# Forgetting gates summed by a scan on turned rows instead of by matmuls, in a two-layer decoder kernel

## The chip, the cores and the metric

The kernel runs on one core of one Trainium2 chip. Its time is the device time of one launch, in microseconds, median of several runs. It works in float32; TensorE gets rounded halves of each operand (a high part and the rest, type fp32r), so every large product is three matmuls.

## The reference

Two decoder layers on an input of 256 rows by 1024 columns. Each layer projects the normalised input to 7428 columns (pool input, queries, keys and values of three attentions, 4 forget logits, 4096 gate logits), runs four mixers, gates and sums them, and then a SwiGLU. What matters here is the forgetting attention with 4 heads:

```
log_f = jax.nn.log_sigmoid(f_logit.astype(jnp.float32) + b_forget.astype(jnp.float32))
cum = jnp.cumsum(log_f, axis=1).transpose(0, 2, 1)
...
logits = (jnp.einsum('bhqd,bhkd->bhqk', qb, k).astype(jnp.float32) * scale
          + cq[..., :, None] - cum[..., None, :])
```

The sum runs over the 256 positions, one per head; the logits need it once by query and once by key.

## The kernel before

**Units.** All large products are cut into 144 units a layer (lists `ITEMS`, `UNITS`). A unit is two slices of 128 rows of a weight matrix by 512 columns, and TensorE does 12 matmuls for it. For each unit SyncE loads 512 KB into one of 6 buffers `raw`, ScalarE writes the rounded part `w_hi` (L884), VectorE writes the rest `w_lo` (L1175), and both wait for a ring of 5: `w_hi` of unit u+4 is written in step u, once TensorE has finished unit u-1. Results stand in `bulk`, two pairs of PSUM banks that items use in turn: the first matmul of an item waits until the item two before has been read out of its bank. The item `gate 6` begins with unit 52, and its bank is given back when VectorE has read item `gate 4` (`gate(layer, 4)`, L1500).

**Order.** Every engine works through its own list, written by hand: `MIXING_PE`, `MIXING_ACT` and `MIXING_DVE` give the step (unit) before which a stage is done. An engine does its stages strictly in that order and waits at each for its semaphores. After the stages of step u, ScalarE and VectorE prepare unit u+4. SyncE's queue carries the weight loads and the trips through device memory (`ROWS_AT`, `PROBS_AT`: steps of going out and of coming back).

**Forgetting gates.** VectorE's `fox_forget` (step 29, L1336) ends the softplus: 128 positions by 8 columns (2 tiles, 4 heads). TensorE's `cum` (step 35, L1711 and L1712) multiplies it by constant triangles, and `cum_evac` on VectorE (step 32 of its list, L1353 to L1357) splits the result into a rounded part and a rest, beside columns of ones that GpSimd filled once. `tr_forget` (step 37, L1695) transposes these rows with four matmuls into bank T, and ScalarE's `forget_evac` (L1034, L1035) copies them as four-row operands `forgetsT` into `queries_hi` and `keys_hi`. `scores("fox", h)` on TensorE (steps 42 and 47) adds the product of these four rows to the scores.

**What follows on ScalarE and VectorE.** `softmax("diff", 3)` and `fox_evac` (steps 38 and 39) prepare the queries and keys of the forgetting attention. Then come `maxima("fox", 0)`, `softmax("fox", 0)`, the copies `o_d` of the differential attention, GpSimd's squares of them (L837), `diff_norm`, `maxima("fox", 1)`, `softmax("fox", 1)`, the three sigmoids of step 48 (L1071), `w_hi` and `w_lo` of unit 52, and `gate(layer, 4)`.

**Turn of the queries.** `turn("dq")` transposes 32 by 32 blocks on VectorE (L1545), SyncE writes them to device memory (L616) and reads them back (L623), and `qk_evac("dq")` reads them in step 23 (ScalarE L962). `lambdas` is three operations on single columns of VectorE.

Of the kernel before, what the change touches and what calls it, by code (L numbers as in the profile page):

```python
# [24 lines left out]
F32 = mybir.dt.float32  # L25
F32R = mybir.dt.float32r
# [6 lines left out]
P = 128  # L33
TT = 2
# [98 lines left out]
def timetable(*entries):  # L133
# [22 lines left out]
def stage_parts(stage, *args):  # L156
# [6 lines left out]
    if stage in ("cum", "pool_a", "pool_b", "tr_forget"):  # L163
        return [((stage,), "T")]
# [26 lines left out]
TURN_AT = {"dq": 13, "dk": 17, "fox": 33, "diff": 48, "merged": 62}  # L191
SPREAD_AT = {}
D0 = LAST[("down", 0)] + 1
ROWS_AT = {"dq": (17, 18), "fox": (36, 37), "diff": (50, 51), "merged": (66, 68), ("ffn", 0): (F0 + 1, F0 + 2), "norm": (D0 + 4, D0 + 5)}
# [8 lines left out]
for _s, _at in PROBS_AT.items():  # L203
# [13 lines left out]
    (32, "softmax", "diff", 1), (34, "probs_evac", "diff", 0), (36, "softmax", "diff", 2), (37, "forget_evac"),  # L217
    (38, "softmax", "diff", 3), (39, "fox_evac", "fq"), (39, "fox_evac", "fk"), (41, "probs_evac", "diff", 1),
# [14 lines left out]
    (37, "probs_turn", "diff", 2), (37, "maxima", "diff", 3), (39, "softmax", "diff", 3), (39, "probs_turn", "diff", 3),
    (39, "fox_evac", "fq"), (39, "fox_evac", "fk"), (40, "gate", 2), (41, "pv_evac", "diff", 1), (41, "maxima", "fox", 0),
    (41, "softmax", "fox", 0), (41, "probs_turn", "fox", 0), (44, "pv_evac", "diff", 2), (44, "gate", 3),
    (45, "pv_evac", "diff", 3), (46, "diff_norm"), (46, "turn", "diff"), (47, "maxima", "fox", 1), (48, "softmax", "fox", 1),
    (48, "probs_turn", "fox", 1), (49, "gate", 4), (49, "pool_evac_b"), (52, "gate", 5), (55, "diff_evac", 1),
    (55, "diff_evac", 0), (56, "gate", 6), (57, "pv_evac", "fox", 0), (57, "pv_evac", "fox", 1), (63, "turn", "merged"),
    (69, "merged_evac", 0), (69, "gate", 7), (71, "merged_evac", 1)]
# [53 lines left out]
def constant_blocks():  # L293
# [6 lines left out]
    blocks["minus_upto"] = (key <= col) * -1.0  # L300
    blocks["minus_ones"] = -np.ones((P, P))
# [20 lines left out]
def build(nc, x, attn_norm, ffn_norm, w_in, b_gate, w_branch, w_out, w_ffn_up, w_ffn_down, consts, params, turned_x, out):  # L322
# [8 lines left out]
    with ExitStack() as ctx:  # L331
# [76 lines left out]
        forget_rows = sb("forget_rows", [P, P + 16], F32, mixing)  # L408
        forget_window = {(w, t): forget_rows[:, 8 * i + 4 * t:8 * i + 4 * t + P] for i, w in enumerate(("fq", "fk")) for t in range(TT)}
# [1625 lines left out]
```

## Time and profile before

| | us |
|---|---|
| median of 3 runs (832.94 to 833.03) | 833.02 |
| the profiled execution | 832.95 |
| its span | 831.1 |
| TensorE busy, 3974 matmuls | 825.6 (99%) |
| VectorE busy | 636.8 (77%) |
| ScalarE busy | 445.8 (54%) |
| GpSimd busy | 200.0 (24%) |

The profiled execution is 1.85 us longer than its span. TensorE's granted clock stands at its upper level (2.4 GHz) in all 40 slices of the page. The two layers follow one another: layer 0 runs to about 411 us of the span, and what layer 0 does at 163 us layer 1 does at 574 us. A line of the timeline gives start, busy time, engine, line, operation, tiles and shapes, how many were merged, and in brackets how long the engine sat idle before it and who released it. Matmuls overlap, so their durations add up to more than the time that passes; the distance between two starts is what a matmul costs TensorE.

### The profile page before, as it was taken

The numbers are of one execution on the slowest core, as the hardware profiler recorded it, in microseconds if no ns is written. First come the engines' busy times: TensorE is split into PE (matmuls) and PEld (weight loads), VectorE is DVE, ScalarE is ACT, GpSimd is POOL, SyncE is SP. The second block draws the span as 40 slices with busy tenths as digits, with TensorE's granted clock in tenths as the row PEclk, the third lists the DMA queues.
The fourth block names the chain that finished last, engine by engine and source line by source line (L and its number), as shares of the span: only waits on it lengthen the run. The fifth ranks groups of instructions, "written<-read, shape, count | busy, mean of one in ns | idle before, by whom it ended". The sixth has DMA issues, their size and how long they took to land.

```text
span 831.1 us, 11025 instructions
## 1 busy us (share of the span) xinstructions
PE 825.6 (99%) x3974; PEld 682.1 (82%) x3974; DVE 636.8 (77%) x958; ACT 445.8 (54%) x642; POOL 200.0 (24%) x285
## 2 busy tenths in 40 slices
PE   9999999999999999999999999999999999999998
PEld 8878788788888888888888888887888888888887
DVE  7899988799687676664679989977986876666652
ACT  6656756654554445444375676566543645444441
POOL 0601201008112333343005102010361133333400
PEclk9999999999999999999999999999999999999999
DMA  9878798686676777676666787886876777776641
GB/s 338 289 227 268 215 293 255 222 280 225 210 239 233 249 214 219 218 228 189 188 216 187 229 252 223 258 275 220 267 243 199 214 244 218 221 219 222 211 141 50
DMA packets 114486, 189.24 MB, mean 228 GB/s; under 512 B 17152, under 2 KB 35072, under 8 KB 114432
## 3 DMA queue, kind: packets, MB, share of 16 engines
q1 hardware_dynamic: 106768, 178.96, 68.3%
q0 software_dynamic: 7232, 8.93, 3.4%
q10 hardware_dynamic: 432, 0.66, 0.3%
q8 instruction: 31, 0.51, 0.2%
q14 instruction: 23, 0.19, 0.1%
HBM read 170.14 MB, written 12.58 MB: 220 GB/s over the span
## 4 chain that ended last, share of the span: by engine, by line
PE 92%; DVE 3%; DMA 2%; ACT 1%; issue 1%; SPq 1%; ACTq 0%; DVEq 0%
PE bulk L1883 29%; PE bulk L1887 29%; PE bulk L1884 29%; DMA raw<-in_w_in_dram 2%; PE bankAB L1676 2%; DVE w_lo L1175 2%; PE bankAB L1792 0%; ACT wide L1071 0%; ACT w_hi L884 0%; PE bankO L1803 0%; PE bankO L1804 0%; PE bankO L1805 0%; PE bankT L1733 0%; SPq L682 0%; SPq L693 0%
## 5 line engine op out<-in xcount | busy, mean ns | idle before, releaser
L1175 DVE TENSOR_TENSOR w_lo<-raw,w_hi 128x1024 fp32r<-128x1024 f32 (+1 forms) x288 | 358.3, 1260 | 110.1 <-ACT w_hi L884 107.5
L884 ACT ACTIVATE w_hi<-raw 128x1024 fp32r<-128x1024 f32 (+1 forms) x286 | 297.0, 1048 | 262.0 <-PE bulk L1887 255.5
L1883 PE MATMUL bulk<-w_hi,hT_hi 128*128 128x512 f32 (+1 forms) x880 | 342.4, 389 | 1.9 <-DVE wide L1286 1.1
L1884 PE MATMUL bulk<-w_lo,hT_hi 128*128 128x512 f32 (+1 forms) x880 | 339.4, 386 | 0.0
L1887 PE MATMUL bulk<-w_hi,hT_lo 128*128 128x512 f32 (+1 forms) x880 | 336.4, 386 | 0.0
L1883 PEld LDWEIGHTS bulk<-w_hi,hT_hi 128*128 128x128 f32 x880 | 165.3, 188 | 36.7 <-issue 2.2
L1887 PEld LDWEIGHTS bulk<-w_hi,hT_lo 128*128 128x128 f32 x880 | 165.0, 188 | 33.3
L1884 PEld LDWEIGHTS bulk<-w_lo,hT_hi 128*128 128x128 f32 x880 | 165.3, 188 | 32.0
L860 POOL DMA_DIRECT2D wide<-wide x192 | 95.0, 504 | 172.1 <-DVE wide L1545 169.7
L846 POOL TENSOR_TENSOR wide<-wide 128x512 f32<-128x512 f32 x24 | 46.1, 1942 | 100.6 <-DVE wide L1510 100.1
L1884 PE MATMUL bulk<-w_lo,aT_hi 128*128 128x512 f32 x174 | 67.8, 389 | 0.0
L1887 PE MATMUL bulk<-w_hi,aT_lo 128*128 128x512 f32 x174 | 67.7, 389 | 0.0
L1883 PE MATMUL bulk<-w_hi,aT_hi 128*128 128x512 f32 x174 | 67.7, 389 | 0.0
L1883 PEld LDWEIGHTS bulk<-w_hi,aT_hi 128*128 128x128 f32 x174 | 32.7, 188 | 6.8
L1887 PEld LDWEIGHTS bulk<-w_hi,aT_lo 128*128 128x128 f32 x174 | 32.7, 188 | 6.7
L1884 PEld LDWEIGHTS bulk<-w_lo,aT_hi 128*128 128x128 f32 x174 | 32.7, 188 | 6.7
L1883 PE MATMUL bulk<-w_hi,oT_hi 128*128 128x512 f32 x80 | 31.4, 392 | 0.0
L1884 PE MATMUL bulk<-w_lo,oT_hi 128*128 128x512 f32 x80 | 31.2, 390 | 0.0
L1887 PE MATMUL bulk<-w_hi,oT_lo 128*128 128x512 f32 x80 | 31.1, 389 | 0.0
L1044 ACT ACTIVATE sb<-bankAB,nmx 128x256 f32<-128x256 f32 x24 | 11.4, 473 | 30.8 <-DVE nmx L1423 30.7
L837 POOL TENSOR_TENSOR wide<-o_d 128x512 f32<-128x512 f32 x4 | 5.9, 1492 | 85.8 <-DVE o_d L1456 85.8
L1528 DVE SCALAR_TENSOR_TENSOR wide<-bulk,y_ffn,wide 128x512 f32<-128x512 f32 (+1 forms) x24 | 15.8, 701 | 10.2 <-ACT wide L1099 10.2
(240 smaller groups left out, 711.3 us busy)
## 6 DMA issues: line engine op xcount, KB each, us to landing
raw<-in_w_in_dram SPq DMA_DIRECT2D x110, 512.0 KB, 4.9
raw<-in_w_ffn_up_dram SPq DMA_DIRECT2D x80, 512.0 KB, 4.6
raw<-in_w_ffn_down_dram SPq DMA_DIRECT2D x44, 512.0 KB, 3.8
raw<-in_w_branch_dram SPq DMA_DIRECT2D x20, 512.0 KB, 5.1
raw<-in_w_out_dram SPq DMA_DIRECT2D x16, 512.0 KB, 3.7
wide<-wide POOLq DMA_DIRECT2D x160, 32.0 KB, 3.3
bias<-in_b_gate_dram SPq DMA_DIRECT2D x16, 256.0 KB, 4.7
raw<-in_w_ffn_up_dram SPq DMA_DIRECT2D x16, 256.0 KB, 3.4
```

Of the source, the lines that this page charges most:

```text
L837: last = pool.tensor_tensor(scratch(t, TA).rearrange("p (h d) -> p h d", h=4), o_d[:, t, :, :], o_d[:, t, :, :], ALU.mult)
L846: ins = pool.tensor_tensor(m, m, wide[:, t, n * D + j * NC:n * D + (j + 1) * NC], ALU.add)
L860: pool.dma_start(spread[b * QUAD:(b + 1) * QUAD, a, :, 0:blocks, :], turned[a * QUAD:(a + 1) * QUAD, b, :, 0:blocks, :]).then_inc(block_sp ...
L884: act.activation(w_hi[:, g % RING, :, 0:width], raw[:, g % RAW, :, 0:width], ACT.Copy).then_inc(hi_ready, 1)
L1044: act.activation(expd[:, m, P:P + SEQ], bank[b][:, P:P + SEQ], ACT.Exp, bias=nmx[:, m:m + 1], accum_out=den[:, m:m + 1])
L1175: vec.tensor_tensor(w_lo[:, g % RING, :, 0:width], raw[:, g % RAW, :, 0:width], w_hi[:, g % RING, :, 0:width].bitcast(F32), ALU.subtract). ...
L1528: vec.scalar_tensor_tensor(out=s, in0=item_bank(layer, ITEM_AT[item], t)[:, 0:width], scalar=y_ffn[:, t:t + 1], in1=s, op0=ALU.mult, op1=A ...
L1676: ins = pe.matmul(dst, a[a_part], b[b_part], start=start and a_part + b_part == 0, stop=stop and a_part == 1, skip_group_check=True)
L1883: pe.matmul(dst, hi, whi, start=(k == ks[0]), stop=False)
L1884: pe.matmul(dst, hi, wlo, start=False, stop=False)
L1887: ins = pe.matmul(dst, lo, whi, start=False, stop=(k == ks[-1] or g == DEPTH * U - 2 and i == 1 and t == 1))
```

## The change

The sum over the positions is no longer made by TensorE.

- `fox_forget` writes the softplus into a 128 x 32 tile and VectorE transposes that in 32 x 32 blocks.
- GpSimd, behind its multiplication `fox_gain` (L823), sends the 128 x 32 tile to device memory, waits for it, and reads it back with 8 transfers so that head h stands on partitions 32h to 32h+3 with all 256 positions in a row (`cumulated`).
- VectorE's new stage `forget_cum`, behind `maxima("diff", 3)`, sums along the row with one scan.
- The new stage `forget_split` on ScalarE (three operations of 128 x 256, the second and third waiting for the first) and on VectorE (three of 128 x 256) makes the rounded part and the rest and writes the four-row operands with signs and ones from a small constant table. It stands behind `softmax("diff", 3)` on ScalarE and behind `fox_evac` on VectorE.
- `cum`, `cum_evac`, `tr_forget` and `forget_evac` are gone.
- `turn("dq")` comes after `qk_norm("dk")` instead of before it, its way out one step later (17 to 18), its way back two (18 to 20); `lambdas` goes from step 10 to step 20.

```diff
-TURN_AT = {"dq": 13, "dk": 17, "fox": 33, "diff": 48, "merged": 62}
+TURN_AT = {"dq": 14, "dk": 17, "fox": 33, "diff": 48, "merged": 62}
...
-ROWS_AT = {"dq": (17, 18), "fox": (36, 37), ...
+ROWS_AT = {"dq": (18, 20), "fox": (36, 37), ...
...
+                pool.wait_ge(forget_turned, nth(forget_turned, layer, "rows"))
+                pool.dma_start(dram_forget.rearrange("a c j -> (a c) j"), forget_rows[:, 1, :]).then_inc(forget_out, 16)
+                pool.wait_ge(forget_out, 16 * nth(forget_out, layer, "rows"))
+                for r in range(4):
+                    for t in range(TT):
+                        pool.dma_start(cumulated[r::QUAD, t * P:(t + 1) * P].rearrange("h (a j) -> h a j", a=NQUAD),
+                                       dram_forget[:, 4 * t:4 * t + 4, :].rearrange("a h j -> h a j")).then_inc(forget_back, 16)
...
-            def forget_evac(layer):
-
-                act.wait_ge(stage_done, nth(stage_done, layer, ("tr_forget",)))
-                act.activation(forgetsT["fq"], bank["T"][:, 0:SEQ], ACT.Copy)
-                act.activation(forgetsT["fk"], bank["T"][:, SEQ:2 * SEQ], ACT.Copy).then_inc(forgetsT_ready, 1)
+            def forget_split(layer):
+
+                act.wait_ge(cum_ready, nth(cum_ready, layer, "cum"))
+                act.wait_ge(stage_done, nth(stage_done, layer, ("scores", "diff", 3)))
+                act.activation(cum_hi, cumulated, ACT.Copy).then_inc(cum_split, 1)
+                act.wait_ge(cum_split, nth(cum_split, layer, "high"))
+                sign, one = c("forget_rows")[:, 0:6:3], c("forget_rows")[:, 2:6:3]
+                for i, which in enumerate(("fq", "fk")):
+                    act.activation(forgetsT[which], cum_hi.bitcast(F32), ACT.Identity, bias=one[:, i:i + 1],
+                                   scale=sign[:, i:i + 1]).then_inc(cum_split, 1)
...
-                vec.scalar_tensor_tensor(out=fg[:, 4, :], in0=fg[:, 0, :], scalar=0.0, in1=fg[:, 3, :],
-                                         op0=ALU.max, op1=ALU.add).then_inc(forget_out, 1)
+                vec.scalar_tensor_tensor(out=softplus, in0=fg[:, 0, :], scalar=0.0, in1=fg[:, 3, :],
+                                         op0=ALU.max, op1=ALU.add).then_inc(vec_step, 1)
+                vec.wait_ge(vec_step, count_step())
+                if layer:
+                    vec.wait_ge(forget_out, 16 * nth(forget_out, layer - 1, "rows"))
+                vec.transpose(forget_rows[:, 1, :], forget_rows[:, 0, :]).then_inc(forget_turned, 1)
...
-            def cum_evac(layer):
...
+            def forget_cum(layer):
+
+                vec.wait_ge(forget_back, 16 * 8 * nth(forget_back, layer, "rows"))
+                vec.tensor_tensor_scan(cumulated, cumulated, cumulated, 0.0, op0=ALU.add, op1=ALU.max).then_inc(cum_ready, 1)
+
+            def forget_split(layer):
+
+                vec.wait_ge(cum_split, nth(cum_split, layer, "high"))
+                vec.tensor_tensor(cum_lo, cumulated, cum_hi.bitcast(F32), ALU.subtract).then_inc(vec_step, 1)
                 vec.wait_ge(vec_step, count_step())
+                sign = c("forget_rows")[:, 1:6:3]
+                for i, which in enumerate(("fq", "fk")):
+                    vec.wait_ge(cum_split, nth(cum_split, layer, "queries" if which == "fq" else "keys"))
+                    last = vec.scalar_tensor_tensor(out=forgetsT[which], in0=cum_lo.bitcast(F32), scalar=sign[:, i:i + 1],
+                                                    in1=forgetsT[which].bitcast(F32), op0=ALU.mult, op1=ALU.add)
+                last.then_inc(forgetsT_ready, 1)
...
-            def tr_forget(layer):
...
-            def cum(layer):
```

Where it lands in the engines' programs. ScalarE of layer 0, before, around step 37: `w_hi` is L884, the softmax of the differential head 3 is L1044 and L1046, `forget_evac` L1034 and L1035, `fox_evac` L1028.

```order
82 L884 ACTIVATE w_hi<-raw 128x1024
83 L1034 ACTIVATE queries_hi<-bankT 128x256
84 L1035 ACTIVATE keys_hi<-bankT 128x256
85 L884 ACTIVATE w_hi<-raw 128x1024
86 L1044 ACTIVATE sb,den<-bankAB,nmx 128x256
87 L1046 ACTIVATE sb,den<-bankAB,nmx 128x128
88 L1044 ACTIVATE sb,den<-bankAB,nmx 128x256
89 L1046 ACTIVATE sb,den<-bankAB,nmx 128x128
90 L884 ACTIVATE w_hi<-raw 128x1024
91 L1028 ACTIVATE queries_hi<-wide 128x2x128 x2
```

The same place now (`w_hi` L891, softmax L1056 and L1058, `forget_split` L1042 and L1046, `fox_evac` L1035):

```order
82 L891 ACTIVATE w_hi<-raw 128x1024 x2
83 L1056 ACTIVATE sb,den<-bankAB,nmx 128x256
84 L1058 ACTIVATE sb,den<-bankAB,nmx 128x128
85 L1056 ACTIVATE sb,den<-bankAB,nmx 128x256
86 L1058 ACTIVATE sb,den<-bankAB,nmx 128x128
87 L1042 ACTIVATE queries_lo<-wide 128x256
88 L1046 ACTIVATE queries_hi<-queries_lo,con 128x256
89 L1046 ACTIVATE keys_hi<-queries_lo,con 128x256
90 L891 ACTIVATE w_hi<-raw 128x1024
91 L1035 ACTIVATE queries_hi<-wide 128x2x128 x2
```

Two operations in front of the softmax have become three behind it, in front of `w_hi` of unit 42.

VectorE of layer 0 at steps 32 and 33, before: `gate 0` (L1500), `cum_evac` (L1353 to L1357), `w_lo` of unit 36 (L1175), the maxima of the differential head 2.

```order
473 L1500 SCALAR_TENSOR_TENSOR wide<-bulk,y_attn,bias 128x512 x2
474 L1353 CAST forget_rows<-bankT 128x2x4
475 L1355 TENSOR_TENSOR forget_rows<-bankT,forget_rows 128x2x4
476 L1357 TENSOR_SCALAR forget_rows<-forget_rows 128x2x4x2
477 L1175 TENSOR_TENSOR w_lo<-raw,w_hi 128x1024
478 L1420 TENSOR_REDUCE row_max<-bankAB 128x2
479 L1421 TENSOR_REDUCE row_max<-bankAB 128x2
```

Now:

```order
472 L1521 SCALAR_TENSOR_TENSOR wide<-bulk,y_attn,bias 128x512 x2
473 L1187 TENSOR_TENSOR w_lo<-raw,w_hi 128x1024
474 L1441 TENSOR_REDUCE row_max<-bankAB 128x2
475 L1442 TENSOR_REDUCE row_max<-bankAB 128x2
```

The three small operations, and the wait for TensorE in front of them, are gone.

VectorE of layer 0 at step 39, before: the end of the softmax, the block transpose of the probabilities (L1579), `fox_evac` (L1399), `w_lo` of unit 43, `gate 2`.

```order
502 L1444 SCALAR_TENSOR_TENSOR probs_room<-sb,inverse,probs_room 128x128
503 L1579 STREAM_TRANSPOSE wide<-probs_room 128x3x4x32
504 L1399 TENSOR_TENSOR queries_lo<-wide,queries_hi 128x2x128 x2
505 L1399 TENSOR_TENSOR keys_lo<-wide,keys_hi 128x2x128 x2
506 L1175 TENSOR_TENSOR w_lo<-raw,w_hi 128x1024
507 L1500 SCALAR_TENSOR_TENSOR wide<-bulk,y_attn,bias 128x512 x2
```

Now:

```order
499 L1465 SCALAR_TENSOR_TENSOR probs_room<-sb,inverse,probs_room 128x128
500 L1600 STREAM_TRANSPOSE wide<-probs_room 128x3x4x32
501 L1420 TENSOR_TENSOR queries_lo<-wide,queries_hi 128x2x128 x2
502 L1420 TENSOR_TENSOR keys_lo<-wide,keys_hi 128x2x128 x2
503 L1372 TENSOR_TENSOR keys_lo<-wide,queries_lo 128x256
504 L1377 SCALAR_TENSOR_TENSOR queries_hi<-keys_lo,con,queries_hi 128x256
505 L1377 SCALAR_TENSOR_TENSOR keys_hi<-keys_lo,con,keys_hi 128x256
506 L1187 TENSOR_TENSOR w_lo<-raw,w_hi 128x1024
507 L1521 SCALAR_TENSOR_TENSOR wide<-bulk,y_attn,bias 128x512 x2
```

Three operations of 256 columns stand between `fox_evac` and `w_lo` of unit 43.

## Rows read from the trace of the kernel before

**Rows 1.** Waits of TensorE, whole span: us in total, times, longest.

```profile
PE bulk L1883 <- DVE wide L1500: 0.8, 2, 0.4
```

**Rows 2.** Timeline of TensorE, layer 0: start, busy, line, shapes, count.

```profile
105.31 0.28 PE L1711 MATMUL bankT<-fg,con 128*128 128x8 f32 x2
...
105.74 0.39 PE L1676 MATMUL bankAB<-keys_hi,queries_hi 64*128 64x256 f32 x2
...
106.59 0.39 PE L1792 MATMUL bankAB<-masks 128*128 128x256 bf16 x2
...
114.13 0.60 PE L1695 MATMUL bankT<-con,forget_rows 128*128 128x128 f32 x4
114.48 0.48 PE L1883 MATMUL bulk<-w_hi,hT_hi 128*128 128x512 f32 x1
...
117.32 0.39 PE L1883 MATMUL bulk<-w_hi,hT_hi 128*128 128x512 f32 x1
...
163.34 0.47 PE L1883 MATMUL bulk<-w_hi,hT_hi 128*128 128x512 f32 x1 [0.41 <-DVE wide L1500]
```

**Rows 3.** Timeline of VectorE, layer 0: the same columns.

```profile
71.84 0.70 DVE L1175 TENSOR_TENSOR w_lo<-raw,w_hi 128x520 fp32r<-128x520 f32 x1 [1.04 <-ACT w_hi L884]
...
95.08 0.70 DVE L1336 SCALAR_TENSOR_TENSOR fg<-fg 128x8 f32<-128x8 f32 x1
...
105.85 0.17 DVE L1353 CAST forget_rows<-bankT 128x8 fp32r<-128x8 f32 x1 [0.86 <-PE bankT L1712]
...
106.35 1.22 DVE L1175 TENSOR_TENSOR w_lo<-raw,w_hi 128x1024 fp32r<-128x1024 f32 x1
107.48 0.68 DVE L1420 TENSOR_REDUCE row_max<-bankAB 128x2 f32<-128x512 f32 x1
...
122.25 1.23 DVE L1175 TENSOR_TENSOR w_lo<-raw,w_hi 128x1024 fp32r<-128x1024 f32 x1 [1.61 <-ACT w_hi L884]
...
124.45 0.48 DVE L1442 SCALAR_TENSOR_TENSOR probs_room<-sb,inverse,probs_room 128x256 f32<-128x256 f32 x1
...
127.04 1.22 DVE L1175 TENSOR_TENSOR w_lo<-raw,w_hi 128x1024 fp32r<-128x1024 f32 x1
...
133.97 0.18 DVE L1433 RECIPROCAL inverse<-den 128x4 f32<-128x4 f32 x1 [1.78 <-ACT sb L1046]
...
145.81 1.28 DVE L1465 TENSOR_REDUCE stat<-wide 128x4 f32<-128x512 f32 x2 [1.93 <-POOL wide L837]
...
161.30 1.23 DVE L1175 TENSOR_TENSOR w_lo<-raw,w_hi 128x1024 fp32r<-128x1024 f32 x1 [2.92 <-ACT w_hi L884]
```

**Rows 4.** Timeline of ScalarE, layer 0.

```profile
71.71 1.14 ACT L962 ACTIVATE queries_hi<-probs_room 128x512 fp32r<-128x512 f32 x2
...
89.78 0.84 ACT L1001 ACTIVATE wide<-bulk,y_attn 128x256 f32<-128x256 f32 x2 [2.23 <-DVE fg L1322]
...
119.55 0.47 ACT L1044 ACTIVATE sb<-bankAB,nmx 128x256 f32<-128x256 f32 x1 [3.17 <-DVE nmx L1423]
...
121.14 1.07 ACT L884 ACTIVATE w_hi<-raw 128x1024 fp32r<-128x1024 f32 x1
...
154.34 0.47 ACT L1044 ACTIVATE sb<-bankAB,nmx 128x256 f32<-128x256 f32 x1 [4.99 <-DVE nmx L1423]
...
157.37 2.96 ACT L1071 ACTIVATE wide<-wide 128x1024 f32<-128x1024 f32 x3
```

**Rows 5.** Timeline of GpSimd, layer 0.

```profile
66.77 2.19 POOL L623 DMA_DIRECT2D wide<-rows_dk  x4 [3.33 <-DMA rows_dk<-wide]
94.64 5.31 POOL L823 TENSOR_TENSOR fox_gained<-wide,parameters 128x256 f32<-128x256 f32 x4 [25.68 <-DVE wide L1286]
```

**Rows 6.** Line L623: from issue to landing.

```profile
DMA to landing us min/median/max: 2.2/3.3/7.1
```

**Rows 7.** Line L1372, VectorE's scans: ns min/median/max.

```profile
L1372 DVE TENSOR_TENSOR_SCAN sb<-sb x16: 392/528/683, 64.5 to 488.6; 128x255 f32<-128x255 f32 x8, 128x127 f32<-128x127 f32 x8
```

**Rows 8.** Timeline of SyncE's queue, layer 0.

```profile
55.83 1.89 SPq L623 DMA_DIRECT2D probs_room<-rows_dq  x4
```

More of the change, by code:

```diff
@@ L229 @@
+    (19, "sb_turn", 0), (20, "lambdas"), (23, "qk_evac", "dq"), (24, "qk_evac", "dk"), (24, "sb_weights", 1),
     (24, "sb_turn", 1), (25, "maxima", "diff", 0), (27, "softmax", "diff", 0), (27, "probs_turn", "diff", 0), (29, "pf"),
     (29, "fox_norm"), (29, "fox_forget"), (30, "maxima", "diff", 1), (31, "sb_evac", 0), (32, "softmax", "diff", 1),
-    (32, "probs_turn", "diff", 1), (32, "sb_evac", 1), (32, "gate", 0), (32, "cum_evac"), (33, "maxima", "diff", 2),
-    (33, "turn", "fox"), (36, "pv_evac", "diff", 0), (36, "gate", 1), (37, "softmax", "diff", 2),
@@ L233 @@
[L233 to L237, printed above, removed]
@@ L238 @@
-    (55, "diff_evac", 0), (56, "gate", 6), (57, "pv_evac", "fox", 0), (57, "pv_evac", "fox", 1), (63, "turn", "merged"),
-    (69, "merged_evac", 0), (69, "gate", 7), (71, "merged_evac", 1)]
+    (32, "probs_turn", "diff", 1), (32, "sb_evac", 1), (32, "gate", 0), (33, "maxima", "diff", 2), (33, "turn", "fox"),
+    (36, "pv_evac", "diff", 0), (36, "gate", 1), (37, "softmax", "diff", 2), (37, "probs_turn", "diff", 2),
+    (37, "maxima", "diff", 3), (37, "forget_cum"), (39, "softmax", "diff", 3), (39, "probs_turn", "diff", 3),
@@ new lines @@
+    (39, "fox_evac", "fq"), (39, "fox_evac", "fk"), (39, "forget_split"), (40, "gate", 2), (41, "pv_evac", "diff", 1),
+    (41, "maxima", "fox", 0), (41, "softmax", "fox", 0), (41, "probs_turn", "fox", 0), (44, "pv_evac", "diff", 2),
+    (44, "gate", 3), (45, "pv_evac", "diff", 3), (46, "diff_norm"), (46, "turn", "diff"), (47, "maxima", "fox", 1),
+    (48, "softmax", "fox", 1), (48, "probs_turn", "fox", 1), (49, "gate", 4), (49, "pool_evac_b"), (52, "gate", 5),
+    (55, "diff_evac", 1), (55, "diff_evac", 0), (56, "gate", 6), (57, "pv_evac", "fox", 0), (57, "pv_evac", "fox", 1),
@@ L243, in evacuations @@
+    (63, "turn", "merged"), (69, "merged_evac", 0), (69, "gate", 7), (71, "merged_evac", 1)]
 def evacuations(mixing, *branches):
@@ L546, in build @@
         forget_ln = signal("forget_ln", ["ln"])
-        forget_out = signal("forget_out", ["softplus", "aug"])
+        forget_turned = signal("forget_turned", ["rows"])
+        forget_out, forget_back = signal("forget_out", ["rows"]), signal("forget_back", ["rows"])
+        cum_ready, cum_split = signal("cum_ready", ["cum"]), signal("cum_split", ["high", "queries", "keys"])
         pooled = signal("pooled", ["pooled"])
@@ L1686, in tr_norm @@
                 ins.then_inc(stage_done, 1)
-            def tr_forget(layer):
-                pe.wait_ge(forget_out, nth(forget_out, layer, "aug"))
-                take("T", forgetsT_ready, layer, "both")
-                for i, which in enumerate(("fq", "fk")):
-                    for t in range(TT):
-                        at = i * SEQ + t * P
-                        ins = pe.transpose(bank["T"][:, at:at + P], forget_window[which, t], identity)
-                ins.then_inc(stage_done, 1)
             def tr_ss(layer):
@@ L1704, in tr_ss @@
                     ins.then_inc(stage_done, 1)
-            def cum(layer):
-                pe.wait_ge(forget_out, nth(forget_out, layer, "softplus"))
-                take("T", forget_out, layer, "aug")
-                sp = fg[:, 4, :]
-                pe.matmul(bank["T"][:, 0:8], c("minus_upto"), sp, start=True, stop=False, skip_group_check=True)
-                ins = pe.matmul(bank["T"][:, 4:8], c("minus_ones"), sp[:, 0:4], start=False, stop=True, skip_group_check=True)
-                ins.then_inc(stage_done, 1)
             def pool_a(layer):
```

58 lines of the change are left out of this document (23 added, 35 removed).

## The prediction, made before the changed kernel ran

> **What bounds the kernel now.** The table of the page comes first: TensorE is busy 99% of the span, so a matmul less is worth its time only where TensorE is never made to wait afterwards. So the second view is TensorE's waits. They are short, but one comes once in each layer and from the same place: 0.41 us until VectorE has read `gate 4` [rows 1, 2]. That is the first matmul of unit 52, at 163.34 us. TensorE was there early; VectorE was late. The third view is therefore the timeline of VectorE, read backwards from there, and what ended each of its idle times.
>
> `w_lo` of unit 52 starts at 161.30, after 2.92 us of idle, released by ScalarE's `w_hi` [rows 3]. ScalarE wrote that behind the three sigmoids of 157.37, these behind a table load and the softmax of 154.34, and that had waited 4.99 us for VectorE's maxima [rows 4]. Before it VectorE idled at 145.81 for GpSimd's squares of a tile that VectorE itself had written, at 133.97 for ScalarE's softmax, and at 122.25 for `w_hi`, which stood behind the softmax that began at 119.55 on VectorE's maxima [rows 3, 4]. None of these waits was ended by TensorE or by a transfer. Going back, the first idle time that TensorE ends is 105.85: 0.86 us for `cum` [rows 3]. So from 105.85 to 163.34 a rigid chain of VectorE, ScalarE and GpSimd runs beside TensorE and is the later of the two when they meet. Call its shift by the change d. TensorE leaves unit 52 d later than before, whatever it saved ahead of it, as long as d is above minus 0.8 (below that its own work binds). Behind unit 52 nothing makes TensorE wait until the next layer, so d is what the layer's time changes by.
>
> **The change part by part.** I work in layer 0; layer 1 has the same wait [rows 1].
>
> *TensorE.* `cum` takes from 105.31 to 105.74, 0.43 us; the four transposes from 114.13 to 114.48, 0.35 us [rows 2]. TensorE is 0.43 us earlier behind step 35 and 0.78 us earlier behind step 37. By the last paragraph this is worth nothing as such: the wait before unit 52 grows by it.
>
> The transposes' rows show 0.60 us for four together [rows 2], while their starts leave 0.35 us to the next product. The Trainium skill ("TensorE: Matmul & The Clock Gate", PE-mode transpose) gives some 275 ns for one transpose of 128 x 128 in a kernel. Four would be 1.1 us an estimate, and the saving 1.5 us a layer; the row disagrees, since these overlap, and the row decides.
>
> *The start of the chain.* VectorE loses 0.86 us of waiting and the three operations of `cum_evac`, which together take from 105.85 to 106.35, 0.50 us [rows 3]. In return the new block transpose stands behind the softplus at 95.08. Its price is not in the trace. Small operations take 0.17 us, but the softplus itself took 0.70 us there, beside GpSimd's multiplication of 94.64 [rows 3, 5]; so 0.2 to 0.7 us, and I take 0.5. Then `w_lo` of unit 36 ends, and the next maxima can start, at 107.48 - 1.36 + 0.5 = 106.6. The maxima also need TensorE's scores, whose last mask matmul began at 106.59, lasted 0.39, and comes 0.43 earlier: 106.55 plus a release [rows 2]. Both say 106.6 to 106.7 instead of 107.48: the chain starts 0.8 us earlier (0.7 to 0.9).
>
> *The scan.* It stands behind `maxima("diff", 3)`, whose successor on ScalarE, the softmax, is not held by it. Scans of 255 elements take at most 0.68 us [rows 7]. It lies in the 1.61 us that VectorE idles ahead of 122.25 [rows 3]; ScalarE needs its result only when the softmax has ended, 1.6 us later. Price 0, and up to 0.7 if that idle time were gone.
>
> *The trip through device memory.* GpSimd ends `fox_gain` at 94.64 + 5.31 = 99.95 [rows 5]. The way out takes an issue of some 0.55 and, as in the rows, 3.3 us of waiting; eight issues at 2.19/4 = 0.55 make 4.4; landing is 3.3 (at most 7.1) [rows 5, 6]. That is 111.5, and 119.1 with both ways at 7.1. The scan asks at 118.7 (0.8 before the 119.55 of the softmax behind the same maxima). Price 0 with 7 us to spare; at the worst 0.4 us. Behind these transfers GpSimd has nothing to do until the squares that release VectorE at 145.81 [rows 3].
>
> *ScalarE's half of the split.* Three operations of 256 columns with factors and offsets from a tile, the second waiting for the first, in front of `w_hi` of unit 42, with nothing ahead to wait for. The nearest row is L1001: two of 256 in 0.84 us [rows 4]. Three are 1.1 us (0.8 to 1.3). The old `forget_evac` stood ahead of the softmax in time that ScalarE spent waiting for the maxima (3.17 us before 119.55 [rows 4]), so its removal gives nothing back. `w_hi` of unit 42 starts at 121.14 - 0.8 + 1.1 = 121.4, and `w_lo`, which waits for it, is 0.3 us late.
>
> *VectorE's half.* Three operations of 256 columns between `fox_evac` and `w_lo` of unit 43 (127.04 [rows 3]), in front of which VectorE does not idle. The row L1442 of the same kind has 0.48 us [rows 3]; less the overlap of starts they are 1.2 us (1.0 to 1.4). Queued behind are `w_lo` of unit 43, `gate 2`, the copy `o_d` and `maxima("fox", 0)`: the whole rest of the chain.
>
> *The forgetting scores of step 42.* TensorE waits there for both halves, which end near 128.6, and could come near 128.2. This wait of some 0.5 us costs nothing by itself; it eats saved time that is lost at unit 52 anyhow.
>
> *The queries' turn and the lambdas.* `turn("dq")` and `lambdas` lie ahead of 105.85, where the chain starts anew, and no TensorE wait follows from them: VectorE idles 1.04 us at 71.84 [rows 3], more than three short operations take. The way back of the queries was issued at 55.83 and is read at 71.71 [rows 4, 8]. Two units later (a unit takes 2.84 us from 114.48 to 117.32 [rows 2]) it is issued near 61 to 63, and lands near 66, at most 70 [rows 6]. Price 0; if it were read late, ScalarE would wait a microsecond or two, and that too before 105.85.
>
> **Sum.** d = -0.8 + 1.1 + 1.2 = +1.5 us a layer; with the ends of the three prices 0.9 to 2.0. Two layers: +3.0 us on the profiled execution of 832.95 us (span 831.1 and 1.85 around it), which stands 0.07 below the median. I forecast 836.0 us, with a range of its own from 834.8 to 837.0.
>
> **The rivals.**
>
> *A, the matmuls' time is kept.* The new operations fall into idle time, d is at or below -0.8, and TensorE keeps 0.78 us a layer: 831.4 us. This is the other side. It decides at unit 52: there the chain must come forward by as much as TensorE does. For it: VectorE does idle 1.61 us just ahead. Against it: that idle time is ScalarE's work seen from VectorE, and the split lengthens just this work; and both halves stand where their engine does not wait.
>
> *B, only one half of the split lies on the chain.* Then d is 0.3 to 0.4, and the time 833.7 us. For it: the scan and ScalarE's half need not be strictly behind each other if ScalarE has idle time that I overlook. Against it: the 121.14 of `w_hi` follows the softmax directly.
>
> *C, the trip through device memory is late.* VectorE is stopped at the scan with everything behind it. If each of the nine issues had to wait for a VectorE operation of 1.2 us (the length of a `w_lo` [rows 3]), they would take 10.8 us in place of 5, the scan would ask before the data had landed at 99.95 + 10.8 + 7.1 + 7.1 = 125, and 6 us more a layer would give 848 us; with half that delay of the issues they land at 119.6, about 1 us late a layer, and the time is 838. Against it: the way of the keys, issued by the same engine, shows 0.55 us for each issue [rows 5]. The Trainium skill ("SBUF — State Buffer", SBUF: two separate sides) states this trap: a transfer issued by GpSimd needs its port to write descriptors, and VectorE can lock it. By that rule C would happen whenever VectorE runs operations that take the port; the four issues of the rows show no such delay.
>
> **Chances.** Forecast 0.80, B 0.08, A 0.07, C 0.05. A measurement of this kernel tells 0.2% (1.7 us) from no change. A ends just at that limit, B inside it; I give faster 0.05, no change 0.14, slower 0.81. The range is 833.9 to 837.4: down nearly to B, up beyond the bounds of d for a short delay by C.
>
> **What would show it.** In the new profile: TensorE's rows of the two groups gone; its wait before unit 52 near 2.2 us instead of 0.41 (0.41 + 1.5 late + 0.78 saved - 0.5 waited at step 42); `w_lo` of unit 42 0.3 us later than 122.25 and of unit 43 1.5 us later than 127.04; GpSimd's last read landed some 7 us before the scan; the scan not preceded by idle time for a transfer. I am wrong if unit 52 starts no later than 163.34, or if a transfer is what ends VectorE's wait.

## The result, and the profile after

The changed kernel takes 836.99 us (median of 6 runs, 836.14 to 839.76), the kernel before 833.00 (6 runs, 832.87 to 833.32). The ratio is 1.0054 with a 95% interval of 1.0044 to 1.0064: slower, as forecast, by 4.0 us where 3.0 were forecast. The median lies in the range, the direction and the place are those of the forecast; 3.1 us of the loss come from the path that the forecast priced (e1 below), and 0.9 us from the part that it priced at nothing. Something else was not foreseen: the runs of the kernel before agree within half a microsecond, those of the changed kernel lie 3.6 us apart.

The profiled execution of the changed kernel took 836.57 us, span 834.7. The page's busy times and its chain by engine:

```profile
PE 824.1 (99%) x3958; PEld 679.5 (81%) x3958; DVE 639.4 (77%) x962; ACT 446.5 (53%) x644; POOL 207.0 (25%) x301
...
PE 86%; DVE 8%; ACT 3%; issue 2%; POOL 1%; ACTq 0%; DVEq 0%
```

TensorE has 16 matmuls less and is busy 1.5 us less, but the chain that ended last passes through other engines for 14% of the span (8% before). Its waits, in the view of [rows 1]:

```profile
PE bankAB L1697 <- DVE keys_hi L1377: 3.1, 2, 2.0
PE bankO L1805 <- DVE o_d L1477: 2.1, 2, 1.0
PE bulk L1885 <- DVE wide L1521: 1.6, 2, 0.8
```

One wait of 0.4 us a layer has become three: for the new split at the forgetting scores of step 42, for a copy at step 45, for `gate 4` at unit 52. All three are releases of VectorE. Its timeline, the places of [rows 3] (maxima of head 2, the scan, `w_lo` of unit 42, the split, `w_lo` of units 43 and 52):

```profile
106.44 0.69 DVE L1441 TENSOR_REDUCE row_max<-bankAB 128x2 f32<-128x512 f32 x1
...
118.39 0.69 DVE L1367 TENSOR_TENSOR_SCAN wide<-wide 128x256 f32<-128x256 f32 x1
...
122.65 1.23 DVE L1187 TENSOR_TENSOR w_lo<-raw,w_hi 128x1024 fp32r<-128x1024 f32 x1 [2.46 <-ACT w_hi L891]
...
127.44 0.42 DVE L1372 TENSOR_TENSOR keys_lo<-wide,queries_lo 128x256 fp32r<-128x256 f32 x1
127.89 0.49 DVE L1377 SCALAR_TENSOR_TENSOR queries_hi<-keys_lo,con,queries_hi 128x256 fp32r<-128x256 f32 x1
128.30 0.48 DVE L1377 SCALAR_TENSOR_TENSOR keys_hi<-keys_lo,con,keys_hi 128x256 fp32r<-128x256 f32 x1
128.69 1.22 DVE L1187 TENSOR_TENSOR w_lo<-raw,w_hi 128x1024 fp32r<-128x1024 f32 x1
...
162.94 1.23 DVE L1187 TENSOR_TENSOR w_lo<-raw,w_hi 128x1024 fp32r<-128x1024 f32 x1 [2.92 <-ACT w_hi L891]
```

Against [rows 3] the maxima start 1.04 us earlier, `w_lo` of unit 42 starts 0.40 later, of unit 43 1.65 later, of unit 52 1.64 later. From unit 43 to unit 52 nothing changed. No row of the chain has a transfer as its releaser, and the scan starts straight behind the maxima. ScalarE's part, where [rows 4] had `w_hi` right behind the softmax:

```profile
120.11 0.43 ACT L1042 ACTIVATE queries_lo<-wide 128x256 fp32r<-128x256 f32 x1
120.57 0.60 ACT L1046 ACTIVATE queries_hi<-queries_lo,con 128x256 fp32r<-128x256 f32 x1
121.08 0.59 ACT L1046 ACTIVATE keys_hi<-queries_lo,con 128x256 fp32r<-128x256 f32 x1
121.57 1.04 ACT L891 ACTIVATE w_hi<-raw 128x1024 fp32r<-128x1024 f32 x1
```

From 120.11 to 121.57 the split holds `w_hi` back for 1.46 us. The sum of layer 0 is -1.04 + 1.46 + 1.24 = +1.66, which is the 1.64 of unit 52.

In layer 1, measured from TensorE's start of its unit 6, the same three terms are -0.76, +1.44 and +1.25, and unit 52 starts 1.95 us later.

GpSimd's trip through device memory (compare [rows 5]):

```profile
98.76 0.60 POOL L835 DMA_DIRECT2D rows_forget<-forget_rows  x1
101.39 4.52 POOL L839 DMA_DIRECT2D wide<-rows_forget  x8 [2.04 <-DMA rows_forget<-forget_rows]
```

The issues of the eight reads end at 105.9, and the last of them lands at 109.4, 9.0 us before the scan.

### The profile page after: what moved, and what is told of

The parts are those of the page before. It is cut to its first block, busy times and chain, and to the rows that moved or that the text cites. A ratio compares the mean times of both kernels' runs of the same rounds, so it can differ in the third digit from the quotient of the medians.

```text
span 834.7 us, 11016 instructions
## 1 busy us (share of the span) xinstructions
PE 824.1 (99%) x3958; PEld 679.5 (81%) x3958; DVE 639.4 (77%) x962; ACT 446.5 (53%) x644; POOL 207.0 (25%) x301
## 4 chain that ended last, share of the span: by engine, by line
PE 86%; DVE 8%; ACT 3%; issue 2%; POOL 1%; ACTq 0%; DVEq 0%
PE bulk L1885 27%; PE bulk L1889 27%; PE bulk L1886 27%; DVE w_lo L1187 2%; DVE wide L1521 1%; PE bankAB L1697 1%; POOL wide L844 1%; ACT w_hi L891 1%; PE bulk L1941 1%; ACT sb L1058 0%; ACT sb L1056 0%; PE bulk L1913 0%; PE bulk L1932 0%; PE bulk L1919 0%; DVE row_max L1441 0%
## 5 line engine op out<-in xcount | busy, mean ns | idle before, releaser
L891 ACT ACTIVATE w_hi<-raw 128x1024 fp32r<-128x1024 f32 (+1 forms) x286 | 296.8, 1047 | 264.8 <-PE bulk L1889 257.1
L1056 ACT ACTIVATE sb<-bankAB,nmx 128x256 f32<-128x256 f32 x24 | 11.4, 474 | 38.7 <-DVE nmx L1444 38.6
```

The costliest lines, as they stand in the source:

```text
L891: act.activation(w_hi[:, g % RING, :, 0:width], raw[:, g % RAW, :, 0:width], ACT.Copy).then_inc(hi_ready, 1)
L1056: act.activation(expd[:, m, P:P + SEQ], bank[b][:, P:P + SEQ], ACT.Exp, bias=nmx[:, m:m + 1], accum_out=den[:, m:m + 1])
```

## The experiments

All were timed in turns with the kernel before, which stood at 832.93, 832.99 and 833.03 us in the three groups (e1 to e4, e5 to e8, e9 to e12). The groups ran on two chips: e1 to e4 on one, e5 to e12 on another.

### e1 and e2: the change in two parts

**e1**, the gates' path alone:

```diff
-TURN_AT = {"dq": 14,          ROWS_AT = {"dq": (18, 20),
+TURN_AT = {"dq": 13,          ROWS_AT = {"dq": (17, 18),
-    (14, "qk_norm", "dk"), (14, "turn", "dq"), ... (20, "lambdas"),
+    (10, "lambdas"), (13, "turn", "dq"), (14, "qk_norm", "dk"), ...
```

> The changed kernel with the queries' turn back at step 13, their rows back at steps 17 and 18 and the lambdas back at step 10: only the forgetting gates' path is changed. Theory 1 (the chain of VectorE and ScalarE work up to unit 52 sets the time, everything ahead of it is slack): TensorE loses the 1.2 us that it gained before unit 16 of layer 0, waits that much less before unit 52 there, and the chain's shift per layer is that of layer 1 of the profiled run, +1.9 us: about 837 us, within 0.5 us of the changed kernel. Theory 2 (the later trip of the queries' rows to device memory is a part of the loss and makes the runs scatter): about 836 us, and the runs agree within 0.5 us where those of the changed kernel scatter over 3.6 us.

**e2**, the same lines the other way round in the kernel before:

> The kernel before with only the queries' turn, their rows' trip and the lambdas moved later; the forgetting gates stay on TensorE. Theory 1: TensorE's wait of 1.1 us before unit 16 of layer 0 goes, but the chain of VectorE starts earlier by no more than its wait for the cumulated sums (0.86 us) and TensorE gives the rest back before unit 52: 832.0 to 833.0 us. Theory 2: the later trip costs, 833.5 us or more, with runs that scatter.

e1: 836.06 us, five runs from 835.94 to 836.33, ratio 1.0038 (1.0026 to 1.0050). e2: 832.65 us, twelve runs from 831.95 to 839.32, ratio 1.0003 (0.9990 to 1.0016). So the gates' path costs 3.1 us, which is the forecast's sum, and its runs lie 0.4 us apart; the scatter belongs to the moved turn. Of the two expectations for e1 the second came true. The first took +1.9 us for each layer; in the profiled execution, counted from unit 6, unit 52 is 1.46 us late in layer 0 and 1.93 in layer 1. For e2 the median fits theory 1 and the scatter of 7.4 us theory 2: neither was whole. Its profiled execution (833.26 us) shows where lost time can come from, the first scores of TensorE waiting for the keys:

```profile
77.87 0.38 PE L1676 MATMUL bankAB<-keys_hi,queries_hi 64*128 64x256 f32 x2 [1.29 <-DVE keys_lo L1392]
```

### e5 and e6: which part of the move

The rows of the queries come back from device memory on SyncE's queue at step 20; GpSimd's queue sends the rows of the keys out at about the same time. **e5** moves the reads alone, in the kernel before:

```diff
-ROWS_AT = {"dq": (17, 18),
+ROWS_AT = {"dq": (17, 20),
```

> The kernel before with one number changed: the reads that bring the queries' rows back from device memory go out at step 20 of SyncE instead of 18, so that they run beside the write of the keys' rows by GpSimd. Theory 2 (the two trips share the DMA engines, the keys' rows land 1 to 3 us later, and in some runs TensorE waits for them at the first scores): runs that scatter over 2 us or more, from 832.9 us to 836 or more, mean 0.5 to 1.5 us above the kernel before. Rival (the turn behind the keys' norm, or the lambdas at step 20, make the scatter): 832.9 us, within 0.5 us in every run.

**e6** takes only that part out of the changed kernel:

```diff
-ROWS_AT = {"dq": (18, 20),
+ROWS_AT = {"dq": (17, 18),
```

> The changed kernel with only the two DMA steps of the queries' rows put back to 17 and 18; the turn stays behind the keys' norm and the lambdas stay at step 20. Theory 2: the reads are over before GpSimd writes the keys' rows, the scatter goes (all runs within 0.6 us), and the median is 836.0 us or up to 0.4 less, since TensorE's gain before unit 16 of layer 0 lets the chain start a little earlier. Rival (the later turn itself, or the trip of the gates' rows, makes the scatter): a median near 837 with runs over 1 us apart.

e5: 833.22 us, eleven runs from 832.85 to 834.39, ratio 1.0004 (0.9995 to 1.0013). e6: 835.46 us, seven runs from 835.12 to 836.07, ratio 1.0028 (1.0018 to 1.0039). e6 speaks for theory 2: with the two DMA steps back the runs lie 0.95 us apart instead of 3.6, though not within the 0.6 expected, and the median is 0.14 below the range expected. So the two DMA steps make the scatter, and neither the later turn nor the lambdas at step 20, which e6 keeps. With early rows the later turn is even worth 0.6 us against e1. e5 fell short of both of its expectations: its runs lie 1.5 us apart, where theory 2 said 2 or more and the rival 0.5, and its mean is 0.4 us above the median of the kernel before. The kernel before had 1.1 us between its own runs in that group, so the times of e5 alone show little.

The rows of the two queues say why the keys come late. In the changed kernel, layer 0, GpSimd's queue and then SyncE's (issue times, and GpSimd's wait for the way out before it asks for the way back):

```profile
61.62 0.76 POOL L619 DMA_DIRECT2D rows_dk<-wide  x1 [18.96 <-DVE wide L1566]
67.23 2.20 POOL L626 DMA_DIRECT2D wide<-rows_dk  x4 [4.85 <-DMA rows_dk<-wide]
...
61.04 1.89 SPq L626 DMA_DIRECT2D probs_room<-rows_dq  x4
```

In e6:

```profile
61.94 0.76 POOL L619 DMA_DIRECT2D rows_dk<-wide  x1 [18.95 <-DVE wide L1566]
66.00 2.19 POOL L626 DMA_DIRECT2D wide<-rows_dk  x4 [3.29 <-DMA rows_dk<-wide]
...
55.72 1.76 SPq L626 DMA_DIRECT2D probs_room<-rows_dq  x4
```

The queries' reads start to be issued 0.6 us ahead of the keys' write instead of 6 us ahead. What this does to the keys' transfers stands in the view of the transfers (KB each, median us from issue to landing). The changed kernel, from 50 to 88 us:

```profile
rows_dk<-wide POOLq DMA_DIRECT2D x1, 512.0 KB, 5.3
wide<-rows_dk POOLq DMA_DIRECT2D x4, 128.0 KB, 3.8
```

and e6:

```profile
rows_dk<-wide POOLq DMA_DIRECT2D x1, 512.0 KB, 3.8
wide<-rows_dk POOLq DMA_DIRECT2D x4, 128.0 KB, 2.9
```

The same view has the queries' reads at 4.0 us here and 2.9 in e6. The other profiled executions say the same. In the six with the reads at step 20 the keys' write took 4.7 to 5.3 us, in both layers. In the eight with the reads at step 18 it took 3.7 to 3.9 us in 14 of 16 cases, and 4.7 in layer 1 of e8 and of e9; so the queries' reads are the main cause of a slow write, but not the only one. The Trainium skill ("DMA: Bandwidth & Descriptors", Queues, rings and completion order) says that one DMA engine serves the queues it has work for in turn, packet by packet. These rows agree that the two queues slow each other, with 1.5 us for a write of 512 KB beside reads of 512 KB; the turns themselves no row shows.

The keys then land when ScalarE already wants them. ScalarE in the changed kernel:

```profile
74.48 1.16 ACT L969 ACTIVATE keys_hi<-wide 128x512 fp32r<-128x512 f32 x2 [1.38 <-DMA wide<-rows_dk]
```

Laid over each other, each layer from one of its first units, the profiled executions of e6 and of the changed kernel agree to 0.06 us in TensorE's starts of layer 1. In layer 0 `w_lo` of unit 28 is 1.40 us later, and units 42 to 60 are 1.2 us later. In the kernel before such a delay went under in the wait for `cum` [rows 3]. In e5 `w_lo` of unit 28 is 0.7 us later, counted from unit 6, and unit 52 0.06 later; of the wait of 0.86 us 0.25 is left:

```profile
105.76 0.17 DVE L1353 CAST forget_rows<-bankT 128x8 fp32r<-128x8 f32 x1 [0.25 <-PE bankT L1712]
```

The change took this wait away, and with it the slack behind which a late transfer could hide. In e2 the delay was larger, and 0.3 us of it reached unit 52.

### e12: the changed kernel once more

> The changed kernel as it is, once more. Theory 2: against the version with the queries' rows at steps 17 and 18 (835.46 us, runs within 0.95 us) it is 1 to 2 us slower and its runs lie over 2 us apart, and in its profile either w_lo of unit 28 comes over 1 us later or the first scores wait for the keys. Rival (its first six runs were chance): median within 0.5 us of 835.5.

839.75 us, five runs from 838.51 to 841.89, ratio 1.0086 (1.0072 to 1.0100): 4.3 us above e6 on the same chip, more than expected, above the range of the forecast, and its shortest run is longer than five of the first six. In its layer 1 the keys' rows released ScalarE after a wait of 1.8 us, TensorE's first scores waited 0.57, and the chain came 1.6 us late to the forgetting scores. There TensorE waited, and what followed was more than the wait (ScalarE's wait for the keys, then TensorE's at the forgetting scores):

```profile
488.23 1.16 ACT L969 ACTIVATE keys_hi<-wide 128x512 fp32r<-128x512 f32 x2 [1.80 <-DMA wide<-rows_dk]
...
542.89 0.58 PE L1697 MATMUL bankAB<-keys_hi,queries_hi 64*128 64x256 f32 x2 [2.00 <-DVE keys_hi L1377]
```

The same stretch by windows (length, busy time and count of PE, PEld, DVE, ACT, POOL, granted clock, DMA share, GB/s):

```profile
538.00:540.00 2.00, 2.00 (x11) 1.49 (x9) 1.92 (x6) 2.00 (x4) 0.00 (x0) 1.00 0.52 200
540.00:542.00 2.00, 0.89 (x7) 0.69 (x6) 1.97 (x6) 0.84 (x1) 0.00 (x0) 1.00 0.26 71
542.00:544.00 2.00, 1.11 (x11) 1.14 (x12) 2.00 (x4) 0.00 (x0) 0.00 (x0) 0.71 0.77 79
544.00:548.00 4.00, 4.00 (x18) 3.12 (x17) 3.54 (x7) 0.39 (x2) 0.00 (x0) 0.50 0.88 306
548.00:552.00 4.00, 4.00 (x16) 3.18 (x15) 2.57 (x8) 4.00 (x12) 0.00 (x0) 0.79 0.81 212
```

After the 2.00 us without work the granted clock fell to 0.50, its lower level (1.2 GHz), for 6.8 us. The unit behind the scores starts 2.6 us later than in e6, the next one 4.7, and at unit 52 it is still 3.15. Of the 3.15 us, 1.6 are the late keys, and I put the other 1.5 down to the clock, by subtraction; no run has the one without the other. The mean clock was 0.994 to 0.998 in all five runs of e12, and 1.000 in all 53 runs of the kernels with the reads at step 18 (e1, e6 to e11). It was 0.994 to 0.996 in four of the changed kernel's first six runs too, the shortest of them (836.14 us) and the longest (839.76) among the four, and 0.996 in the longest run of e2; in all runs of e3, e4 and e5 it was 1.000. So only kernels with late reads show the fall, not all of them do, and a fall does not have to make a run long. In the first profile a wait of the same 2.0 us, in layer 0, left the clock at 1.00, so the wait alone does not decide it. The Trainium skill ("TensorE: Matmul & The Clock Gate", What's actually happening) puts the clock down to how busy TensorE has been lately. The rows of e12 agree, with TensorE busy 0.89 of 2.00 us before the fall.

### e3 and e10: VectorE's half of the split

```diff
 def forget_split(layer):          # VectorE
-    vec.wait_ge(cum_split, nth(cum_split, layer, "high"))
-    vec.tensor_tensor(cum_lo, cumulated, ...)
-    ... two scalar_tensor_tensor into forgetsT
+    vec.wait_ge(cum_split, nth(cum_split, layer, "keys"))
+    vec.tensor_copy(nmx[:, 0:1], nmx[:, 0:1]).then_inc(forgetsT_ready, 1)
```

e3 is this edit in the changed kernel, e10 the same in e6.

> The changed kernel without VectorE's half of the split: the low parts of the cumulated sums are left out of the four rows (one operation of 4 elements stands in for the three of 256). Theory 1: the 1.24 us per layer of that half stand on the chain to unit 52, so it is 2 x 1.2 = 2.4 us (2.0 to 2.6) faster than the changed kernel, near 834.6. Rival (VectorE has slack there and the loss comes from the trip through device memory or from the clock): as the changed kernel within 0.5 us.

> The version with the queries' rows at steps 17 and 18 (835.46 us) without VectorE's half of the split: the low parts of the cumulated sums are left out of the four rows. The first try of this was clouded by the late rows. Theory 1: 2 x 1.24 us less, 833.0 us (832.7 to 833.3), with runs within 0.6 us. Rival (the half isn't on the path): 835.4.

e3: 834.60 us, eleven runs from 833.62 to 838.33, ratio 1.0026 (1.0017 to 1.0036). It is 2.4 us below the first median of the changed kernel, but with 4.7 us between its runs this shows little. e10: 832.97 us, eleven runs from 832.74 to 833.36, ratio 1.0000 (0.9991 to 1.0008): 2.49 us less than e6, 1.24 a layer, where 127.44 to 128.69 in the rows above is 1.25. (Laid over each other, the two profiled executions say 1.15 a layer; the small operation that stands in has a price too.)

### e4, e7 and e8: the same operations where their engines wait

The scan goes ahead of the softmax of head 2, ScalarE's half ahead of the exponentials of head 3 (5.8 us of waiting for the maxima), VectorE's half behind `w_lo` of unit 41 (2.5 us of waiting for `w_hi`):

```diff
 MIXING_DVE
-    (37, "maxima", "diff", 3), (37, "forget_cum"), ... (39, "fox_evac", "fk"), (39, "forget_split"),
+    (36, "forget_cum"), (37, "softmax", "diff", 2), ... (37, "maxima", "diff", 3), (38, "forget_split"),
 MIXING_ACT
-    (38, "softmax", "diff", 3), (38, "forget_split"),
+    (38, "forget_split"), (38, "softmax", "diff", 3),
 forget_split on ScalarE
-    act.wait_ge(stage_done, nth(stage_done, layer, ("scores", "diff", 3)))
+    act.wait_ge(stage_done, nth(stage_done, layer, ("scores", "diff", 2)))
```

e4 is this in the changed kernel, e7 in e1, e8 in e6.

> The changed kernel with the scan moved ahead of the softmax of head 2 (before it behind the maxima of head 3), ScalarE's half of the split ahead of the exponentials of head 3, where ScalarE waited 5.8 us, and VectorE's half behind w_lo of unit 41, where VectorE waited 2.5 us for w_hi of unit 42. Theory 1: of the chain's terms only the scan's 0.69 us is left beside the -1.04 of its start, so unit 52 starts 0.35 us per layer earlier than in the kernel before: 832.3 us (831.7 to 833.0), faster than both. Rival (the trip through device memory lands too late for a scan at 114 us in some runs, or the loss isn't these halves): 835 us or more, with scatter.

> The forgetting gates' path of the changed kernel with the queries' turn, rows and lambdas as before, and with the scan and both halves of the split moved into the idle times of ScalarE (5.8 us ahead of the exponentials of head 3) and VectorE (2.5 us ahead of w_lo of unit 42). Theory 1: per layer 1.46 + 1.24 us leave the chain and the scan's 0.69 us enters it, against the version with old turns and the split on the chain (836.06 us): 836.06 - 2 x 2.01 = 832.0 us (831.7 to 832.7), within 0.5 us in every run, 0.9 us faster than the kernel before. Rival (the chain to unit 52 is only as short as in the kernel before, because something else ends there): 832.9 us.

> As the one before, but with the queries' turn behind the keys' norm and the lambdas at step 20, the queries' rows at steps 17 and 18. Theory 1 and 2 together: TensorE loses the wait of 1.1 us before unit 16 of layer 0 and no run is late: 831.6 us (831.2 to 832.2), within 0.6 us in every run. Rival: as the one before or slower, with scatter.

e4: 832.61 us, eleven runs from 831.53 to 835.53, ratio 1.0000 (0.9992 to 1.0009), the median inside the range expected, with the scatter of the late reads; it was expected to be faster than the kernel before and is not. e7: 831.90 us, eleven runs from 831.62 to 832.02, ratio 0.9986 (0.9977 to 0.9995). e8: 830.99 us, nine runs from 830.86 to 831.33, ratio 0.9975 (0.9966 to 0.9985). e7 is 4.2 us below e1, where 4.0 were expected; e8 is 4.5 below e6 and 0.2 below the range expected for it. In e8 ScalarE runs its half in its waiting time, and 3 us of waiting are left ahead of the exponentials:

```profile
113.21 0.42 ACT L1042 ACTIVATE queries_lo<-wide 128x256 fp32r<-128x256 f32 x1 [0.81 <-DVE wide L1367]
...
117.77 0.47 ACT L1056 ACTIVATE sb<-bankAB,nmx 128x256 f32<-128x256 f32 x1 [3.01 <-DVE nmx L1444]
```

Of the new operations behind the maxima of head 2, only the scan is left on the chain. The same operations that cost 3.1 us in the order of e1 gain 1.1 in that of e7.

### e9: is TensorE's time worth anything?

Into e6, TensorE gets work of the removed size back, into a bank that nobody reads:

```diff
+    (35, "extra", 0), (35, "scores", "diff", 2), ... (37, "scores", "diff", 3), (37, "extra", 1),
+    extra 0: two matmuls into bank T, 8 and 4 columns;  extra 1: four transposes of 128 x 128
```

> The changed kernel with the queries' rows at steps 17 and 18 (835.46 us), and TensorE given work of the size of the removed one back, into a bank that nobody reads: two small matmuls ahead of the scores of head 2, four transposes behind the scores of head 3. Theory 1 (TensorE has slack there): the transposes' 0.43 us per layer cost nothing; the matmuls' 0.35 us count only by what VectorE waits for the scores of head 2 (0.15 us in layer 1, none in layer 0), so 0 to 0.35 us per layer: 835.5 to 836.1. Rival (TensorE's time is the kernel's time): 2 x 0.78 more, 837.0 us.

836.14 us, five runs from 835.97 to 836.36, ratio 1.0038 (1.0025 to 1.0050): 0.68 above e6, at the upper end of the 0 to 0.7 expected. Laid over e6, TensorE is 0.35 us late behind the small matmuls and 0.78 behind the transposes, and from step 42 on 0.4 (0.37 in layer 1). So the transposes cost nothing. The small matmuls cost their full 0.35 us a layer, because the maxima of head 2 wait for the scores behind them, in layer 0 too, where none was expected:

```profile
105.79 0.69 DVE L1443 TENSOR_REDUCE row_max<-bankAB 128x2 f32<-128x512 f32 x1 [0.50 <-PE bankAB L1807]
```

### e11: the rest of the chain

In e8, ScalarE's three sigmoids of step 48 go behind `w_hi` of unit 52:

```diff
-    (48, "softmax", "fox", 1), (48, "sigmoid", 0, 1), (48, "sigmoid", 1, 0), (48, "sigmoid", 1, 1),
-    (49, "pool_evac_b"),
+    (48, "softmax", "fox", 1),
+    (49, "pool_evac_b"), (49, "sigmoid", 0, 1), (49, "sigmoid", 1, 0), (49, "sigmoid", 1, 1),
```

> The version with the early split and the queries' rows at steps 17 and 18 (830.99 us), and ScalarE's three sigmoids of step 48 (2.96 us and a table load of 1.28) put behind w_hi of unit 52 and the pooled rows, at step 49. Theory 1: the chain that ends at unit 52 loses 4.2 us, more than TensorE waits there (1.2 us of w_lo or gate 4 per layer at most), so TensorE's wait before unit 52 goes: 0.4 us for the chain's part and up to 0.8 more per layer: 829.4 us (828.8 to 830.4). Rival (another wait, for VectorE's gate 4 or the gates of the branches, ends there): 830.9 us or more.

828.93 us, five runs from 828.83 to 829.24, ratio 0.9951 (0.9939 to 0.9964), inside the range expected and faster than both kernels. `w_hi` of unit 52 comes 4.3 us earlier, the unit itself 0.95, the next 1.09. What stays in the list of TensorE's waits is the one at the start of the program:

```profile
PE bulk L1941 <- DVE warm L1625: 1.0, 1, 1.0
```

## Why the forecast was right in direction and too small

- **The chain and its end at unit 52: shown.** From the maxima of head 2 to unit 52 the rows shift as a block, all of e1's loss on it is made between 105 and 129 us and at the same place of layer 1, and taking operations off this stretch gives their length back (e10, e7, e8), as does taking ScalarE's sigmoids off its end (e11).
- **TensorE's saving worth nothing by itself: shown for the transposes (e9).** The 0.35 us ahead of the scores of head 2 do count, as the forecast's start of the chain had it. The forecast's two sizes, 0.43 for `cum` and 0.35 for the transposes, are distances between starts in the rows. Laid over each other, e9 and e6 say 0.35 and 0.43, and the kernels before and after say 0.34 and 0.44; the sum is the same, and a distance between two starts was good to 0.1 us.
- **Start of the chain, -0.8:** -1.04 in layer 0, -0.76 in layer 1. The block transpose took 0.21 us, below the 0.5 taken.
- **ScalarE's half, +1.1 with an upper bound of 1.3: too small,** 1.46 and 1.4. This is the one priced term that was mis-sized. I took the duration of a plain operation for all three. The two that read factor and offset from a tile take 0.60 us instead of 0.43. They are also of another function (Identity instead of Copy), and no run separates the two. The Trainium skill ("ScalarE: Activation LUTs", What ACT_TABLE_LOAD costs) gives 186 ns and 0.833 ns a column, the same for every function, and some 93 ns more for each such operand. By that page it is 0.40 and 0.59 us, an estimate, and the rows have 0.43 and 0.60.
- **VectorE's half, +1.2:** 1.24 and 1.25, and 1.24 again by e10.
- **Sum +1.5 a layer:** +1.46 and +1.93 in e1, the latter at the upper end of the bounds. The time of e1, 3.1 us above the kernel before, is the forecast's 3.0, in part by luck: before unit 5 the profiled e1 is some 0.3 us shorter, and its layer 0 has 0.46 us from a shorter wait before unit 16.
- **The scan and the gates' own trip, price 0: shown** by the rows; rival C did not happen. The eight issues took 4.52 us, 0.56 each, beside a VectorE that was never idle, so the trap named in the forecast does not show here. The milder case of rival C was mis-summed: nine issues in 5.4 us are only 0.4 us above the forecast's own 5, and half of the delay would be 7.9 us, data at 122.1, and some 843 us.
- **The queries' turn and the lambdas, price 0: this is the step that failed.** It had two faults. It looked only at when the queries' rows are read, and not at what their transfer runs beside: it is the keys' rows that came late. And it called everything ahead of 105.85 free because "the chain starts anew" there, in the trace of before. That fresh start was the wait for `cum`, which the change removes. In place of 0 the whole move costs 0.9 us (first six runs against e1). The two DMA steps in it cost 1.5 us (first six runs against e6), and 4.3 us in the last group (e12 against e6, one chip), where the low clock adds to it. The later turn with early rows gains 0.6 us (e6 against e1). In the profiled executions TensorE's wait of 1.1 us before unit 16 of layer 0 is gone in e6. That wait was in the profile of before, and the forecast didn't look at it:

```profile
PE bulk L1883 <- DVE wide L1286: 1.1, 1, 1.1
```

- **The range: in part luck.** The bounds of the sum end at 837.0, and the range went on to 837.4 for a short delay of the gates' own trip, which did not happen. What filled the upper part was the keys' trip, which the forecast did not price, and the kernel's runs in the last group (839.75) lie above the range.
- **The signs named in advance.** `w_lo` of unit 42 +0.40 (0.3 said), of unit 43 +1.65 (1.5 said). The wait before step 42 was 1.1 and 2.0 us where 0.5 was said, and one at step 45 was not named, so less was left for unit 52 (0.8 where 2.2 was said). GpSimd's last read landed 9.0 us before the scan (7 said). In layer 0 the three waits make 2.0 + 1.0 + 0.8 = 3.8 us; 0.4 of before, 1.6 late, 0.8 saved and the 1.1 that TensorE no longer waits before unit 16 make 3.9.

Open is why the changed kernel was slower in the last group than in its first runs, and why the clock fell after one wait of 2.0 us and not after another. Several of the comparisons above (e6 against e1, e7 against e1, the first six runs against e6) are between groups; the kernel before stood within 0.1 us in all of them.

## What to carry to other kernels

When a change removes a wait, ask what used to disappear in it: the wait was also the slack of everything ahead. Price a moved transfer by what it then runs beside, on every queue, and not only by when its own data are read. And where two engines meet late, the place of an operation counts for more than its length: the same six operations and a scan made the kernel 3.1 us slower behind the maxima and softmax of head 3, and 1.1 us faster in the waits ahead of them.

## What the runs showed of the hardware

- A write of 512 KB and four reads of 128 KB on two queues slow each other: the write took 3.8 us without the reads and 5.3 beside them, the reads 2.9 and 4.0, and the reads that follow the write 2.9 and 3.8 (e6 and the changed kernel, layer 0).
- A single wait of TensorE of 2.0 us was followed by 6.8 us at the lower clock in one execution (e12) and by none in another; the lower clock came with some 1.5 us on top, by subtraction.
- Four transposes of 128 x 128 took 0.43 us of TensorE's time when put back (e9), some 0.11 us each.
- A VectorE scan over 256 elements takes 0.69 us, a block transpose of 128 x 32 takes 0.21 us.
